# Decoder trunk: output projections, first and last MLP groups and gates in two token halves

## The reference, cut to what matters

```python
for i in range(2):
    hn = rms_norm(h, norm_mix_pre[i])
    mix = even_mixer(hn, ...) if i == 0 else odd_mixer(hn, ...)   # attention, ends in o @ w_out
    h = h + rms_norm(mix, norm_mix_post[i])
    hn = rms_norm(h, norm_mlp_pre[i])
    m = square(relu(hn @ w_mlp_up[i])) @ w_mlp_down[i]            # 1024 -> 4096 -> 1024
    h = h + rms_norm(m, norm_mlp_post[i])
    gate = sigmoid(rms_norm(h, ple_norm[i]) @ w_ple_gate[i])
    h = h + gate * (p[i] @ w_ple_proj[i])                         # p[i]: 1024 x 256
```

## Time and profile before

| | |
|---|---|
| median of three runs | 3223.07 us (3221.32 to 3223.57) |
| span of the profiled execution | 3221.5 us, which is its own time: between 3221.32 and 3223.57 it agrees with the runs |
| PE busy in matmuls | 2919.4 us, 91% |
| PE weight loads (beside the matmuls) | 2385.4 us, 74% |
| DVE / ACT / POOL busy | 1331.0 / 860.2 / 952.7 us |
| stages (PE): out 0, MLP 0, ple and gate 0, odd input | from 614, 721, 1449 and 1599 us |
| the same in layer 1: out 1, MLP 1, ple and gate 1 | from 2290, about 2350 and 3081 us |

### The profile page before, as it was taken

The page is one execution under the profiler, slowest core; times in us unless marked ns, Lnnn a source line. Parts: engine busy times, 40 slices in busy tenths (PEclk is TensorE's granted clock), DMA queues, the critical chain, the costliest instruction groups (busy, mean ns, idle before and its releaser), DMA issues.

```text
span 3221.5 us, 37112 instructions
## 1 busy us (share of the span) xinstructions
PE 2919.4 (91%) x13684; PEld 2385.4 (74%) x13684; DVE 1331.0 (41%) x1905; ACT 860.2 (27%) x1581; POOL 952.7 (30%) x622
## 2 busy tenths in 40 slices
PE   8896888889999999999999976867889999999999
PEld 5785777767888888876788865757658888888867
DVE  4625777325222222227433147787272222222264
ACT  3204766322110000024200035756331000011141
POOL 2320144342332332252232202131423223323342
PEclk9998999999999999999999986879989999999999
DMA  4236432211111111111235264544201111111112
GB/s 154 109 126 178 124 80 66 79 40 33 46 52 46 46 47 51 46 53 53 79 124 218 79 162 102 120 103 120 79 33 46 52 46 46 48 50 46 59 35 77
DMA packets 73791, 253.66 MB, mean 79 GB/s; under 512 B 9699, under 2 KB 13283, under 8 KB 73367
## 3 DMA queue, kind: packets, MB, share of 16 engines
q1 hardware_dynamic: 58728, 196.35, 20.5%
q10 hardware_dynamic: 14944, 55.74, 4.5%
HBM read 203.99 MB, written 52.78 MB: 80 GB/s over the span
## 4 chain that ended last, share of the span: by engine, by line
PE 75%; DVE 15%; issue 4%; ACT 3%; DMA 2%; POOL 1%; SPq 0%; DVEq 0%; ACTq 0%; POOLq 0%
PE ACC L1035 62%; PE OP L1197 3%; PE ACC L1167 3%; PE TR L1181 3%; DVE R L1634 2%; DVE T L1657 1%; DVE H L1660 1%; DVE PT L1783 1%; PE OP L1091 1%; DVE XL L1640 1%; ACT PT L1431 1%; PE TR L1210 1%; DVE T L1682 1%; DVE PB L1772 1%; DVE HL L1685 1%
## 5 line engine op out<-in xcount | busy, mean ns | idle before, releaser
L873 POOL CAST WH<-RAW 128x1024 fp32r<-128x1024 f32 x203 | 215.9, 1064 | 1575.5 <-PE ACC L1035 1554.6
L1035 PE MATMUL ACC<-XH,WH 128*128 128x512 f32 x1792 | 575.0, 402 | 72.3 <-DVE XL L1640 38.5
L1035 PE MATMUL ACC<-XL,WH 128*128 128x512 f32 x1792 | 556.4, 392 | 0.0
L1035 PE MATMUL ACC<-XH,WL 128*128 128x512 f32 x1792 | 555.4, 391 | 0.0
L875 POOL TENSOR_TENSOR WL<-RAW,WH 128x1024 fp32r<-128x1024 f32 x203 | 495.2, 2439 | 24.8 <-POOL WH L873 1.5
L1035 PEld LDWEIGHTS ACC<-XH,WH 128*128 128x128 f32 x1792 | 337.3, 189 | 172.8 <-issue 89.6
L1035 PEld LDWEIGHTS ACC<-XL,WH 128*128 128x128 f32 x1792 | 339.2, 189 | 71.8
L1035 PEld LDWEIGHTS ACC<-XH,WL 128*128 128x128 f32 x1792 | 338.8, 189 | 71.7
L1393 ACT ACTIVATE HH<-T 128x1024 fp32r<-128x1024 f32 x64 | 67.9, 1061 | 1168.6 <-DVE T L1682 1168.6
L1689 DVE TENSOR_TENSOR M<-M,ACC 128x1024 f32<-128x1024 f32 x128 | 156.3, 1221 | 496.1 <-PE ACC L1035 496.1
L1035 PE MATMUL ACC<-HH,WH 128*128 128x512 f32 x1024 | 316.8, 391 | 17.0 <-DVE HL L1685 17.0
(11 more groups left out here) (192 smaller groups left out, 3466.8 us busy)
## 6 DMA issues: line engine op xcount, KB each, us to landing
RAW<-in_w SPq DMA_DIRECT2D x203, 512.0 KB, 3.4
QK<-y_odds SPq DMA_DIRECT2D x128, 256.0 KB, 5.2
y_odds<-HALVES ACTq DMA_DIRECT2D x16, 1024.0 KB, 5.2
QK<-y_foxs SPq DMA_DIRECT2D x48, 256.0 KB, 5.4
y_foxs<-HALVES ACTq DMA_DIRECT2D x8, 1024.0 KB, 5.2
y_kv<-Q ACTq DMA_DIRECT2D x8, 512.0 KB, 2.6
BIAS<-y_f SPq DMA_DIRECT2D x8, 512.0 KB, 7.7
H<-in_xT ACTq DMA_DIRECT2D x8, 512.0 KB, 7.3
```

What stands on the lines that cost most here:

```text
L873: nc.gpsimd.tensor_copy(WH[:, slot], RAW[:, slot]).then_inc(s_whi, 1)
L1035: mm = nc.tensor.matmul(acc[:, h * HALF:(h + 1) * HALF], w(k), x[:, k, h * HALF:(h + 1) * HALF], start=first and k == k0 and w is ws and x ...
```

## The change

Five things are done at once.

1. **Two token halves.** `out0`, `out1`, `mlpa`, `mlpz`, `gate` and `in1p` run all their units for tokens 0 to 511 and then all again for tokens 512 to 1023. A half tile takes one bank of the four (`banks`), so up to four are open. A unit's weights are fetched and split once in each half. The norms m, h, n, g and x1 are computed for each half by itself (`stats_half`, `root_half`, `inverse_half`).
2. **One half's norm beside the other's products.** The queues are rewritten in the new `layer_end` of each engine: m's first half is applied beside out's second, its second half beside the first half's up units; n's first half beside mlpz's second, its second beside `ple`; g's second beside the gates of the first. Layer 0 and layer 1 differ in the places (`early`).
3. **Squares pre-summed.** For h, g and x1 DVE adds the squares of chunks 1 to 6 to chunk 0's (in the memory of M), for n too; for m POOL does. PE then multiplies by ones twice for a half instead of eight times for the whole.
4. **Down units.** In every MLP group the first unit's two tiles run all terms but the last, and then each its last.
5. **Smaller moves.** M's first group is copied from PSUM by ACT (`down0`) in place of memset and add. The odd layer's operands go to XH and XL instead of buffers of their own; P is fetched in two pieces into `PRAW` and split into HH and HL; the stream's copy `y_h` is written by ACT after the gates; the output is stored in half chunks.

```diff
 def unit_plan():
+    def halves(name, *units):
+        segs.append((name, 1, len(units), [(k, src, made, h, w) for h in range(2)
+                                           for w, (k, src, made) in enumerate(units)]))
...
     def rest(l):
+        halves(f"mlpa{l}", *ups, *downs("down0"))
+        whole(f"mlp{l}", N_GROUPS - 2, *ups, *downs("down"))
+        halves(f"mlpz{l}", *ups, *downs("down"))
+        whole(f"ple{l}", 1, *[(2, "p", tiles_of(*[("ple", 4 * a + j) for j in range(4)])) for a in range(2)])
+        halves(f"gate{l}", *[full("gate", c) for c in range(DC)])
...
@@ POOL
-            weights("out0", lambda pos: sum_squares("m0", range(pos - 2, pos - 1)))
+            weights("out0", lambda pos: sum_squares(0, range(pos - 2, pos - 1)))
+            sum_squares(0, range(14, 16))
...
-            weights("out1", lambda pos: sum_squares("m1", range(2 * pos - 4, 2 * pos - 2)))
+            weights("out1", lambda pos: sum_squares(1, range(2 * pos - 4, 2 * pos - 2)))
+            sum_squares(1, range(12, 16))
...
@@ PE, weights
+                        last = u.k - 1
+                        if u.src == "hid" and u.tiles[0].idx == 0:
+                            for m in range(2):
+                                for k in range(last):
+                                    product(m, k)
+                            for m in range(2):
+                                product(m, last)
...
@@ PE, layer_end: stats_half(name, half) runs after these tiles (kind, half, index)
+                places = {("out", 1, 0 if early else 1): (m, 0)}
+                if early:
+                    places["out", 1, 7] = h, 0
+                weights(f"out{l}", after=then_stats(places))
+                places = {("up", 0, 0 if early else 2): (m, 1), ("down0", 0, 6 if early else 7): (h, 1)}
+                if not early:
+                    places["up", 0, 1] = h, 0
+                weights(f"mlpa{l}", operand_ready(h, "up"), then_stats(places))
+                weights(f"mlp{l}", hid_ready)
+                weights(f"mlpz{l}", hid_ready, then_stats({("up", 1, 0): (n, 0), ("down", 1, 7): (g, 0)}))
...
+                weights(f"ple{l}", after=then_stats({("ple", None, 1): (n, 1)}))
+                places = {("gate", 0, 2): (g, 1)}
+                if l == 0:
+                    places["gate", 1, 6] = "x1", 0
+                weights(f"gate{l}", operand_ready(g, "gate"), then_stats(places))
...
@@ DVE
+            def residual(name, h, cs, then):
+                for c in cs:
+                    x = M[:, c, half(h)]
+                    V_.scalar_tensor_tensor(out=x, in0=x, scalar=GAINS[:, GAIN[name], c:c + 1],
+                                            in1=R[:, half(h)], op0=ALU.mult, op1=ALU.mult).then_inc(s_T, 1)
+                    dve.wait_ge(s_T, scaled[name, h] + c + 1)
+                    V_.tensor_tensor(H[:, c, half(h)], H[:, c, half(h)], x, ALU.add).then_inc(s_res, 1)
+                    if c:
+                        low_h(then, h, c - 1)
+                    if c == DC - 1:
+                        low_h(then, h, c)
...
@@ DVE, layer_end
+                inverse_half(m, 0)
+                dve.wait_ge(s_evA, out.half(0)[-1].act)
+                residual(m, 0, range(DC), h)
+                sum_squares(h, 0, range(1, 7))
+                inverse_half(h, 0)
+                up = first.half(0)[:HID_GROUP]
+                if early:
+                    inverse_half(m, 1)
+                    dve.wait_ge(s_evA, out.half(1)[-1].act)
+                    for t in up:
+                        evacuate(t)
+                        residual(m, 1, range(2 * t.idx, 2 * t.idx + 2), h)
+                else:
+                    evacuate(up[0])
+                    evacuate(up[1])
+                    inverse_half(m, 1)
+                    dve.wait_ge(s_evA, out.half(1)[-1].act)
+                    evacuate(up[2])
+                    residual(m, 1, range(2), h)
+                    evacuate(up[3])
+                    residual(m, 1, range(2, DC), h)
+                sum_squares(h, 1, range(1, 7))
+                inverse_half(h, 1)
...
+                up, down = last.half(1)[:HID_GROUP], last.half(1)[HID_GROUP:]
+                evacuate(up[0])
+                inverse_half(n, 0)
+                evacuate(up[1])
+                residual(n, 0, (0, 1), g)
+                evacuate(up[2])
+                residual(n, 0, (2, 3), g)
+                evacuate(up[3])
+                for t in down:
+                    if t.idx < 4:
+                        residual(n, 0, (4 + t.idx,), g)
+                    if t.idx == 4:
+                        dve.wait_ge(s_phi, l + 1)
+                        V_.tensor_tensor(HL[:, :, half(0)], PRAW[:, :, half(0)],
+                                         HH[:, :, half(0)].bitcast(F32), ALU.subtract).then_inc(s_p, 1)
+                    evacuate(t)
+                    sum_down(n, 1, t.idx - 1)
+                    if 4 <= t.idx < 7:
+                        sum_squares(g, 0, range(2 * t.idx - 7, 2 * t.idx - 5))
+                inverse_half(g, 0)
+                inverse_half(n, 1)
+                residual(n, 1, range(DC), g)
+                sum_squares(g, 1, range(1, 7))
...
```

More of the change, by code:

```diff
@@ L46, in unit_plan @@
 def unit_plan():
-    full = lambda kind, idx, step=0, src="x": (8, src, [(kind, idx, step)])
-    mlp = [full("up", c) for c in range(HID_GROUP)]
-    mlp += [(4, "hid", [("down", 2 * j, 0), ("down", 2 * j + 1, 0)]) for j in range(DC // 2)]
+    tiles_of = lambda *kinds: [(kind, idx, 0) for kind, idx in kinds]
     segs = []
-    def rest(l):
[L57 to L61, removed]
@@ L79, in unit_plan @@
+    halves("in1p", full("odds", 0), full("odds", 1), full("odd", 6), full("odd", 7))
+    whole("in1a", 5, full("odds", 2, 2), full("odds", 3, 2))
+    whole("in1b", 3, full("odd", 0, 2), full("odd", 1, 2))
+    whole("in1c", 1, *[full(kind, c) for kind, c in (("odds", 12), ("odds", 13), ("oddk", 14), ("oddk", 15))])
+    halves("out1", *[(4, "x", tiles_of(("out", 2 * a), ("out", 2 * a + 1))) for a in range(4)])
     rest(1)
@@ L126, in __init__, with tile @@
         self.name, self.n, self.iters = name, n, iters
+        self.half = lambda h: [t for u in iters[0] if u.h == h for t in u.tiles]
 def build_segments(extra_before):
     segs, extras, tiles, units = {}, {}, [], []
[L134 to L138, removed]
+    w_base = 0
+    def tile(kind, idx, h=None):
+        t = Tile(kind, idx, len(tiles), tiles[-1] if tiles else None, h)
+        for x in reversed(tiles[-4:]):
+            if set(x.banks) & set(t.banks):
+                t.before = x.no
+                break
+        t.summed = [x.dve for x in tiles[-40:] if x.kind == "down" == kind and x.idx == idx]
+        tiles.append(t)
+        return t
+    for name, n, n_w, body in unit_plan():
         extras[name] = [tile(*x) for x in extra_before.get(name, [])]
@@ L688, in _, with weights @@
             load_h(sp, 0)
[L690 removed]
+            def weights(name, after=None):
                 seg = segs[name]
@@ L1276, in _ @@
             layer_end(0)
-            weights("in1p", **first_unit("x1", range(7)))
+            weights("in1p", operand_ready("x1", "odds"), then_stats({("odd", 0, 7): ("x1", 1)}))
             for name in ("in1a", "in1b"):
@@ new lines, in hidden, with down0 @@
+                def hidden(t):
+                    mlp([t], 0)
+                def down0(t):
+                    act.wait_ge(s_tile, t.no + 1)
+                    nc.scalar.activation(M[:, t.idx, t.cols], acc(t), ACT.Copy).then_inc(s_evA, 1)
+                out, first, last = segs[f"out{l}"], segs[f"mlpa{l}"], segs[f"mlpz{l}"]
+                for t in out.half(0):
+                    mixed(t)
+                beside = {1: [0], 2: [1, 2], 3: [3, 4], 4: [5, 6], 5: [7]} if early else \
+                    {4: [0, 1], 5: [2], 6: [3, 4], 7: [5, 6, 7]}
@@ new lines, in layer_end @@
+                for t in out.half(1):
+                    mixed(t)
+                    if t.idx == (0 if early else 1):
+                        root_half(m, 0)
+                    stream(h, 0, beside.get(t.idx, ()), m)
+                root_half(h, 0)
+                up, down = first.half(0)[:HID_GROUP], first.half(0)[HID_GROUP:]
+                if early:
+                    root_half(m, 1)
+                    beside = {0: [0, 1], 1: [2, 3], 2: [4, 5], 3: [6]}
+                else:
+                    beside = {2: [0, 1], 3: [2]}
@@ new lines, in layer_end @@
+                for t in up:
+                    hidden(t)
+                    if t.idx == 1 and not early:
+                        root_half(m, 1)
+                    stream(h, 1, beside.get(t.idx, ()), m)
+                beside = {0: [7]} if early else {c: [c + 3] for c in range(5)}
+                for t in down:
+                    down0(t)
+                    stream(h, 1, beside.get(t.idx, ()), m)
+                root_half(h, 1)
```

(10 more changed lines are left out.)

648 lines of the change are left out of this document (355 added, 293 removed).

## The result

The changed kernel takes 3258.8 us (median of four, 3253.7 to 3261.1) against 3223.3 us of the kernel before (now a median of four as well): ratio 1.0108, 95% interval 1.0094 to 1.0121. It is 35 us slower where 33 us less were forecast, and lies above the range. The profiled execution has a span of 3259.3 us, 37.8 more than that of before.

What follows compares the result with a forecast made beforehand. The prediction took the kernel to be a PE matmul stream losing time waiting for norms: 104.2 us gain without contention, less 71 for DVE and POOL taking turns, leaves 33, so 3223.1 becomes 3190 us; range 3120 to 3221.

Steps and rivals of the forecast that it cites:

- the group loop: MLP groups: the new order of down units removes PE's wait for DVE's HL, saving 14.5 us.
- the port: Half stages: DVE operations on two SBUF tensors and POOL's reading operations take turns, costing 71 us of the gain.
- A to D: Stretches: out 0 (A) or 1 (C) to whole groups, then layer ends (B, D); PE time beyond products, 65.7 us uncontended.
- Contention: Half stages: the part pricing POOL instructions that must pass inside DVE chains, 88.7 us in full, 71 taken.
- 2.0 and 1.6 in the gates: Gates in B and D: DVE's delay from taking turns with POOL, 2.0 and 1.6 us.
- the sum without the port: Whole kernel: excess falls from 169.9 to 65.7 us if DVE and POOL never take turns, a gain of 104.2.
- full price: Half stages: DVE and POOL take strict turns throughout, costing 88.7 us.
- I take 0.8 of it, 71: Half stages: 88.7 us cut to 71, as evacuation and ACT work before a DVE operation can cover part of a split.
- Rival 2: PE's waits for h, g and HL in mlpa, mlpz: many short waits survive, TensorE's clock falls; 3235 us, chance 0.08.
- Rivals 1 (the port doesn't bind): Half stages: DVE slips through POOL's free time or catches up during PE's waits; gain 104, 3119 us, chance 0.27.
- 3 (doubled fetches bind): Half units: weight landing rises beyond 7.4 us; 1 us of surplus costs 64 us, giving 3250; chance 0.02.
- Rival 4: Whole kernel: the halves bring nothing and only the loop's 14.5 us stay, 3209 us; chance given only jointly with another case.

Runs made afterwards that it cites:

- experiment 7: Changed kernel with POOL's weight cast and subtraction replaced by memsets in the half units of out, mlpa and mlpz only: 3185.9 us.
- experiment 6: Changed kernel with POOL's weight cast and subtraction replaced by memsets in the half units of the gates and in1p only: 3212.8 us.
- experiment 2: Changed kernel with POOL's weight cast and subtraction replaced by memsets of about equal length in all half units: 3146.2 us.
- experiment 8: Against the kernel of experiment 2, layer 1's last three POOL adds of m's squares moved behind mlpa's first two splits: 3149.6 us.

## Why the prediction was wrong

*Right:* statistics at 1.72 us a half norm; the group loop (14.5 forecast, 13.6 measured alone); weights and fetches at no price of their own; the port as what speaks against the sum, with turns in the rows of before. Without the port A to D were forecast at 65.7 us of excess and came to 91.7.

*The step that failed* is a term of "Contention", "2.0 and 1.6 in the gates". The mechanism was right, DVE and POOL taking turns; its price in these stages was put at 3.6 us and is 46. The other miss is the sum without the port. The price of the port by stages (us):

| stages | full price | at 0.8 of it | measured |
|---|---|---|---|
| `out`, first and last MLP groups | 85.1 | 68 | 73 (experiment 7) |
| gates, odd projections | 3.6 | 3 | 46 (experiment 6) |
| all | 88.7 | 71 | 113 (experiment 2) |

The gates' term was put down without a count of splits; the prediction shows none. The trace has five beside the chain of g's second half (1489 to 1521 us), some 17 us of POOL's reading beside 30 DVE operations that last from 1488.0 to 1523.5. And it had no price for a missed edge: PE waits 6.2 us in each layer and 9.6 and 5.6 for x1, and each time 3.75 us of statistics run at the lower level in place of 1.72. Experiment 6 removes these: by its trace B's excess falls from 63.1 to 34.3 us and D's from 46.8 to 36.7. The three waits of B with their slow statistics are 27.5 of its 28.8, the one of D 8.2 of its 10.1.

The credit, "I take 0.8 of it, 71", is not what failed. In `out` and the MLP it stands 5 us under the measured price. By stretch (after less experiment 2) the port cost 24.6 us in A, where the full price was 25.9, but 22.5 in C, where it was 31.2. So strict turns were nearly the right reading for A, where DVE's chain has a backlog all through, and too dear for C. That the reason given for the credit holds, evacuations and ACT's work between DVE's operations, no run shows. Of A's price 5.4 us are not a DVE chain at all: out 0 lasts 96.3 us where it lasts 90.8 without the port, since PE waits for a split (2.9 us before 708.31) and runs slowly behind it; the prediction had some 4 for this.

Together the port cost 113 us where 71 were taken, 42 of the miss of 69. The rest, 27 us, is the sum without the port, which was 3119 and measured 3146. Of these 26 lie in the four stretches: 3.4, 4.8, 13.7 and 4.1 from A to D. In C the prediction had "nothing lost" at the first up tile, and PE waits 6.6 us there; it counted no matmuls at the lower clock, of which C has some 6 us (experiment 8). About 1.8 of A's 3.4 are such matmuls too: its first 216 take 50.99 us where 0.2276 each are 49.2. The rows of before had shown them: the first 192 of out 1 take 45.65 us for 43.7. In B and D g's first statistics are 9.4 us late (6.6 forecast), with 2 us of slow statistics behind (experiment 2). Why they are late by 2.8 us more than forecast was not followed up.

*Slips in the sums*, none of which matters here: A's first chain loses 31.9 less 13.2, 18.7 and not 18.3 us; C's three splits and five adds are 16.8 and not 16.0; and 3155, called the port at 0.6 of its price, is 0.4 of it, while 0.6 gives 3172.

*The rivals.* Rival 2 named the right side, and h's and g's places though not x1's. Its price for the clock was too high (27 forecast, 16 measured) and its time, 3235, still 24 us too low, since it built on the same full price of the port (88.7 where 113 were measured). It was given 0.08, because "today's excess holds the same loss already"; the trace of before has one such row of slow statistics beside its long waits, the changed kernel eight of 3.75 us. Rivals 1 (the port doesn't bind) and 3 (doubled fetches) are both refuted by experiment 2. Rival 4, "only the loop's 14.5 us stay", was still too kind: the halves took 50 us back (3258.8 against 3208.4).

## What to carry to other kernels

Splitting work in two to hide a chain doubles what is done once per piece. If that work (here POOL's splitting of weights) takes turns with the engine of the chain, it lengthens the chain that it was to cover: add the two demands in each stage before counting anything as hidden, in every stage. Here the stages that were counted came out at 73 us for 85, and the one that was put down without a count at 46 for 3.6. A wait that is just missed costs more than its length, since the clock falls in it (each of eight statistics took 2.0 us more); where sums may be late, place what waits for them one piece of independent work further back (34 us here). Try the small independent parts of a large change alone: the order of the down units and x1's summed squares were worth 26 us, and were buried in it.

## What the runs showed of the hardware

- `scalar_tensor_tensor` with two SBUF tensors takes turns with POOL's cast and subtraction just as `tensor_tensor` does: 1232 and 1082 ns beside them (scale, H), 745 and 708 with POOL memsets of the same total length in their place; an add of PSUM to SBUF isn't touched (682 and 683 ns).
- After 16 small multiplications (3.7 us, granted clock 1.00) and 4.9 us of idling PE ran the statistics at its lower level (0.50, 1.2 GHz); where 35 of them (8.0 us) left 0.7 us idle it stayed at 1.00: 3.78 against 1.98 us for the same statistics.
